# Padding the pitch of the stationary tiles of an fp32r matmul stream: 1040 and 1028 bytes in place of 1024

## What is computed

```python
f = swiglu(rmsnorm(h, ffn1_pre_g), ffn1_w_gate, ffn1_w_up, ffn1_w_down)   # (silu(x@Wg) * (x@Wu)) @ Wd
h = h + 0.5 * rmsnorm(f, ffn1_post_g)
z = rmsnorm(h, mix_pre_g) @ w_in
# head group A: gelu(gate) * RG-LRU(causal_conv4(x_a)); head group B: B * causal_conv3(C * x_b)
h = h + rmsnorm(concat(A, B) @ w_out, mix_post_g)
f = swiglu(rmsnorm(h, ffn2_pre_g), ffn2_w_gate, ffn2_w_up, ffn2_w_down)
h = h + 0.5 * rmsnorm(f, ffn2_post_g)
```

## Time and profile before

| | us |
|---|---|
| median of 2 runs | 1818.22 (1818.16 to 1818.27) |
| span of the profiled execution, first to last instruction | 1816.7 |
| TensorE busy, share of the span | 99% |
| VectorE, ScalarE busy | 52%, 47% |
| granted TensorE clock, mean over the span | 0.998 of 2.4 GHz |

### The profile page before, as it was taken

How to read it: one execution, slowest core, us unless ns; L and a number is a source line. 1 busy time by engine, 2 the same in 40 slices (tenths; PEclk the granted TensorE clock), 3 DMA queues, 4 the chain that set the end, 5 groups by cost and what they waited for, 6 DMA issues and landing times.

```text
span 1816.7 us, 22683 instructions
## 1 busy us (share of the span) xinstructions
PE 1799.5 (99%) x8066; PEld 1486.2 (82%) x8066; DVE 940.9 (52%) x990; ACT 847.9 (47%) x1023; POOL 20.2 (1%) x21
## 2 busy tenths in 40 slices
PE   8999999999999999999999999999999999999998
PEld 6888888888888888788888878888888888888886
DVE  5545444454454445655686465545445445445444
ACT  6544444444434334566654456444444444434442
POOL 0000000000000000100000010000000000000000
PEclk9999999999999999999999999999999999999999
DMA  7666666666565566675565656666666666556554
GB/s 229 215 191 193 190 188 193 186 188 192 176 199 189 171 203 204 188 211 173 164 196 174 199 160 231 186 189 192 185 186 191 189 187 192 176 177 216 189 184 148
DMA packets 179189, 344.69 MB, mean 190 GB/s; under 512 B 10685, under 2 KB 12869, under 8 KB 178757
## 3 DMA queue, kind: packets, MB, share of 16 engines
q1 hardware_dynamic: 179108, 344.04, 60.7%
q10 hardware_dynamic: 32, 0.01, 0.0%
HBM read 341.91 MB, written 2.10 MB: 189 GB/s over the span
## 4 chain that ended last, share of the span: by engine, by line
PE 98%; ACT 0%; DVE 0%; DMA 0%; issue 0%; POOL 0%; DVEq 0%; SPq 0%; ACTq 0%
PE ps L858 32%; PE ps L860 32%; PE ps L859 32%; PE ps L945 1%; PE ps L894 1%; PE ps L986 0%; PE ps L998 0%; DMA resid<-in_x 0%; DVE xT_lo L617 0%; ACT xT_hi L405 0%; POOL rstd L340 0%; ACT w_hi L383 0%; ACT act_g L387 0%; DVE resid L607 0%; DVEq L96 0%
## 5 line engine op out<-in xcount | busy, mean ns | idle before, releaser
L583 DVE TENSOR_TENSOR w_lo<-raw,w_hi 128x1024 fp32r<-128x1024 f32 x636 | 776.5, 1224 | 824.2 <-ACT w_hi L383 821.2
L383 ACT CAST w_hi<-raw 128x1024 fp32r<-128x1024 f32 x640 | 670.3, 1053 | 853.6 <-PE ps L860 829.5
L858 PE MATMUL ps<-w_hi,xT_hi 128*128 128x512 f32 x1728 | 679.0, 393 | 2.5 <-DVE xT_lo L617 2.5
L860 PE MATMUL ps<-w_hi,xT_lo 128*128 128x512 f32 x1728 | 674.0, 390 | 0.0
L859 PE MATMUL ps<-w_lo,xT_hi 128*128 128x512 f32 x1728 | 673.4, 390 | 0.0
L858 PEld LDWEIGHTS ps<-w_hi,xT_hi 128*128 128x128 f32 x1728 | 325.0, 188 | 69.1 <-issue 3.3
L860 PEld LDWEIGHTS ps<-w_hi,xT_lo 128*128 128x128 f32 x1728 | 324.9, 188 | 68.5
L859 PEld LDWEIGHTS ps<-w_lo,xT_hi 128*128 128x128 f32 x1728 | 325.1, 188 | 66.2
L858 PE MATMUL ps<-w_hi,hT_hi 128*128 128x512 f32 x832 | 327.5, 394 | 0.0
L860 PE MATMUL ps<-w_hi,hT_lo 128*128 128x512 f32 x832 | 326.3, 392 | 0.0
L859 PE MATMUL ps<-w_lo,hT_hi 128*128 128x512 f32 x832 | 323.6, 389 | 0.0
(11 more groups left out here) (77 smaller groups left out, 314.7 us busy)
## 6 DMA issues: line engine op xcount, KB each, us to landing
raw<-in_ffn_w_gate SPq DMA_DIRECT2D x176, 512.0 KB, 4.4
raw<-in_ffn_w_up SPq DMA_DIRECT2D x176, 512.0 KB, 3.5
raw<-in_ffn_w_down SPq DMA_DIRECT2D x176, 512.0 KB, 4.8
raw<-in_w_in SPq DMA_DIRECT2D x80, 512.0 KB, 3.8
raw<-in_w_out SPq DMA_DIRECT2D x32, 512.0 KB, 4.8
resid<-in_x SPq DMA_DIRECT2D x8, 256.0 KB, 8.8
gpost<-in_ffn_post_g SPq DMA_DIRECT2D x2, 1024.0 KB, 6.5
out<-resid SPq DMA_DIRECT2D x8, 256.0 KB, 2.8
```

The costliest lines, as they stand in the source:

```text
L383: sc.copy(w_hi[:, s], raw[:, s]).then_inc(hi_ready, 1)
L583: ve.tensor_tensor(w_lo[:, s], raw[:, s], w_hi[:, s].bitcast(f32), ALU.subtract).then_inc(lo_ready, 1)
L858: te.matmul(dst, xh, w_hi[:, s, k], start=start and k == 0, stop=False)
L860: last = te.matmul(dst, xl, w_hi[:, s, k], start=False, stop=stop and k == GK - 1)
```

## The change

xT_hi and xT_lo get four more elements in each row of 256 (pitch 1040 bytes), hT_hi and hT_lo one more (pitch 1028 bytes); the added elements are never read or written. Tile (k, t) so starts at 1040 k + 512 t, or 1028 k + 512 t. The region is moved so that its distance from the start of the ring is a multiple of 512 bytes; tiles in it start at multiples of 32 bytes. The two accesses that took whole rows of hT (lines 551 and 823) name the 256 elements. Loops, instructions, waits and their order stay.

```diff
+        ring_at = (nc.sbuf_base + 31) // 32 * 32
         raw = sb("raw", [P, SLOTS, GK, W])
         w_hi = sb("w_hi", [P, SLOTS, GK, W], f32r)
         w_lo = sb("w_lo", [P, SLOTS, GK, W], f32r)
-        xT_hi = sb("xT_hi", [P, KD, T], f32r)
-        xT_lo = sb("xT_lo", [P, KD, T], f32r)
+        xT_hi = sb("xT_hi", [P, KD, T + 4], f32r)
+        xT_lo = sb("xT_lo", [P, KD, T + 4], f32r)
...
-        region_at = (nc.sbuf_base + 31) // 32 * 32
-        region_size = 4 * 2 * KF * T
-        sb("region", [P, 2 * KF * T])
+        line = 512
+        first = (nc.sbuf_base + 31) // 32 * 32
+        region_at = first + (ring_at - first) % line
+        region_size = 4 * 2 * KF * (T + 1) + 32
+        sb("region", [P, (region_at - first + region_size) // 4])
...
-            return nc.alloc_sbuf_tensor_at(name, shape, dt, offset=region_at + offset), offset + size
-
-        hT_hi, o = at("hT_hi", [P, KF, T], 0, f32r)
-        hT_lo, o = at("hT_lo", [P, KF, T], o, f32r)
-
-        o = 4 * KD * T
+            return nc.alloc_sbuf_tensor_at(name, shape, dt, offset=region_at + offset), (offset + size + 31) // 32 * 32
+
+        hT_hi, o = at("hT_hi", [P, KF, T + 1], 0, f32r)
+        hT_lo, o = at("hT_lo", [P, KF, T + 1], o, f32r)
+
+        o = 4 * KD * (T + 1)
...
-        assert o <= 4 * KF * T
-        o = 4 * KF * T + 4 * KD * T
+        assert o <= 4 * KF * (T + 1)
+        o = 4 * (KF + KD) * (T + 1) + 16
...
-                    sc.copy(hT_hi[:, MC * n:MC * n + MC, :], yy[:]).then_inc(y_hi, 1)
+                    sc.copy(hT_hi[:, MC * n:MC * n + MC, 0:T], yy[:]).then_inc(y_hi, 1)
...
-                    ve.tensor_tensor(hT_lo[:, MC * n:MC * n + MC, :], yy[:],
-                                     hT_hi[:, MC * n:MC * n + MC, :].bitcast(f32), ALU.subtract).then_inc(y_lo, 1)
+                    ve.tensor_tensor(hT_lo[:, MC * n:MC * n + MC, 0:T], yy[:],
+                                     hT_hi[:, MC * n:MC * n + MC, 0:T].bitcast(f32), ALU.subtract).then_inc(y_lo, 1)
```

## The result

The changed kernel takes 1854.15 us (1853.97 to 1854.34, 2 runs) against 1818.22 before: 1.020 times as long, with a 95% interval of 1.018 to 1.022. The forecast was 1821, the range 1742 to 1848. The kernel is slower, by 35.9 us, and outside the range.

What follows compares the result with a forecast made beforehand. The prediction took TensorE, through the spacing of its 7680 product matmuls, to bound the kernel. xT at +5.2 and hT at -2.5 us, all else 0, gave +2.7 on 1818.2, called 1821, with a range of 1742 to 1848.

Steps and rivals of the forecast that it cites:

- writers and waits: ScalarE and VectorE writes of the moved tiles, and TensorE's waits for them: 0 taken, at most doubled.
- this reading: xT and hT products: their 2.0 ns difference in spacing comes from the tile offset; both at 0.2268 would save 5 us.
- the lone products: Four TensorE products thought to have no weight load beside them took 0.39 or 0.40 us, evidence against loads costing 11 ns.
- the gap of 11 ns: Product spacing of 0.2268 us with xT against 0.2159 for line 998's matmuls, which read their moving operand at half rate.
- faster: Rival on product spacing: the two operand reads collide at equal offsets and different offsets part them; 1729 or 1774, chance 0.33.
- Loads from odd starts: Rival on hT weight loads at pitch 1028: starts off multiples of 16 bytes lengthen them; +187 us, chance 0.05.
- the price of an unseen offset: Spacing of xT and hT products at their new offsets, taken as 0.2278 us: +5.2 us and -2.5 us.
- the two settled spacings: Product starts in undisturbed TensorE stretches before the change: 0.2268 us apart with xT, 0.2288 with hT.
- the higher value: hT's spacing of 0.2288 us at offset 448; leaving that offset was to save 2.5 us.
- six starts: xT products from 840.51 to 841.90, behind line 998: 1.39/6 = 0.232 us apart, used as the upper bound for unsettled spacing.
- the offsets never settle: Rival on product spacing: each offset step disturbs it, 0.2315 us throughout; +31 us, 1849, chance 0.14, half over 2%.
- the prize: All products brought down to a spacing of 0.2159 us: 89 us saved, the most the change could gain.

Runs made afterwards that it cites:

- the aligned kernel: Against the kernel before: pitch 1024 everywhere, only the region moved so that hT too stands at offset 0 modulo 512; 1812.14 us, ratio 0.9969.

## Why the prediction failed

**What held.** TensorE's spacing was the only thing to look at; nothing was added, writers and waits cost nothing (predicted 0, seen 0), and the loads stayed at 188 ns. The difference between xT and hT before was the offset, as read: the aligned kernel gave 5.7 us, and this reading had priced 5. What was concluded from the lone products held: the gap of 11 ns is not given back by moving tiles, and the rival "faster" with its 0.33 got nothing in any of sixteen kernels (no spacing below 226.7). Two of the four, those with hT tiles, were not quite alone: the transposes' loads start at 743.48 and 1070.41, beside their last 0.13 us. "Loads from odd starts" had no part: a load takes 188 ns on average at every offset, 4 and 8 included, and 190 at 48.

**The step that failed** is the price of an unseen offset: "I take the middle of the two settled spacings, 0.2278, as the row pair nearest to 'another offset'", for xT +5.2 us and for hT -2.5. Measured: xT +26.3, hT +11.0. Two values of a function of the offset said nothing about the rest of it. The two that the kernel before happened to use, 0 and 192 modulo 256, are the best and the fourth best of the fourteen known; the ten that are worse lie between 230.7 and 234.3. Leaving the offset that shows "the higher value" made hT worse, because 448 was a good one.

**The better row was there.** Behind line 998 six starts gave 0.232, a spacing of the same products out of step. That was the only row of a state other than the two settled ones, and it was right within 1 ns for xT and 2 for hT. It was priced as the rival "the offsets never settle", +31 us against 35.9 measured, with a chance of 0.14, half of it over 2%. Its size was nearly right, and its mechanism too as far as it went: in the changed kernel the spacing does not settle, and even the tiles at the offsets 0, 16, 192 and 240 are at 232. What it missed is that a constant offset can settle and be just as slow. The six starts are 1.39/6 = 0.2317 apart, the bounds say 0.232, and the rival was priced with 0.2315; with 0.232 it comes to +35, 1853. The upper end of the range, 1848, was 1 us under that rival's own 1849, with nothing for its error; with the 0.2336 that the changed kernel's count showed for hT (90.39/387), for both stages, it would have been 1818 + 5184 x 0.0068 + 2496 x 0.0048 = 1865.

**Small slips in the sums** that change nothing above: both stages at 0.2268 give 1813, not 1812; five sixths of the prize end at 1744, not 1742; 3 x 4 x 0.7 is 8.4, not 8.6.

**What stays open.** Why the spacing depends on the distance within 256 bytes, and why on this irregular map, is not shown. It needs products back to back at the 2.4 GHz level; whether it acts through the load beside a product was not separated. What makes the base gap of 11 ns is not shown either; it is absent at 1.2 GHz and with line 998's operand, and the lone products speak against the load beside them. A stream of products without loads, with the stationary tile kept, would separate the load from the neighbouring product and was not run.

## What to carry over

In an fp32r matmul stream like this one (512 columns, one load per matmul), try the stationary tiles and the moving operand at the same address modulo 256, with pitches that leave it so (1024 did). Here no other offset was better, and a pad that moves tiles off a power of two was what cost time. When a change moves an operand to addresses that the trace has never seen, two observed values are two samples: run the map, or let the range reach to the worst spacing that any row shows, disturbed stretches included. And take a change apart before it is judged: its alignment alone gained 0.3%, the pitch of 1040 lost 1.4%, and the pitch of 1028 lost 0.9% against the aligned kernel.

## Unexpected behaviour of the hardware

- The spacing of fp32r products with 512 columns at 2.4 GHz follows a pattern that repeats: at offset 0 it is 226 or 227, 226.7 in the mean; at 448 and 192 a turn of three (232, 226, 229); at 64 a turn of two (236, 231); at 128 a turn of seven. Behind transposes it takes up to ten products to come back to it. At the 1.2 GHz level it is 426.7 at the offsets 0, 4 and 32 alike.
- It depends on the distance between the stationary and the moving tile modulo 256 bytes, by up to 7.5 ns (3.3%); two pairs 256 bytes apart agree, and moving both operands by 64 changed nothing. Changing the distance every three products, or within them, costs up to 5.7 ns where a constant one is good. The Trainium skill, "SBUF — State Buffer", section "Who interferes with whom", has TensorE waiting for no one and its two reads independent. By that rule the distance between the two operands should not matter, and the map, 226.8 to 234.3, does not agree; whether one read holds up the other was not shown.
- A shorter stationary tile can slow the stream down: with 64 columns in place of 128 for one product in three, loads of 135 in place of 188 ns, the spacing rose by 3 ns.
